# A depthwise convolution of 31 taps: VectorE's taps of the first and last channel group summed in SBUF, and the taps of a few groups shared out anew

## The reference

```
def _conv_module(h, w1, b1, wdw, bdw, lng, lnb, w2, b2):
    a, gt = jnp.split(h @ w1 + b1, 2, axis=-1)
    u = a * jax.nn.sigmoid(gt)
    u = lax.conv_general_dilated(
        u, wdw[:, None, :], window_strides=(1,),
        padding=[(CONV_WIDTH_2 // 2, CONV_WIDTH_2 // 2)],
        dimension_numbers=('NWC', 'WIO', 'NWC'),
        feature_group_count=u.shape[-1]) + bdw
    u = jax.nn.silu(_layernorm(u, lng, lnb))
    return u @ w2 + b2
```

## Time and profile before

| | us |
|---|---|
| median of 3 runs | 2614.68 (2612.6 to 2616.1) |
| the profiled execution's own time | 2617.16 |
| its span, first to last instruction | 2615.1 |
| TensorE busy | 2499.9 (96%) |
| VectorE busy | 1745.0 (67%) |
| ScalarE busy | 1092.4 (42%) |
| GpSimd busy | 366.2 (14%) |

### The profile page before, as it was taken

One profiled execution on the slowest core, in us unless ns is written; L12 is line 12 of the kernel. 1 busy time (PEld: TensorE's weight loads), 2 busy tenths in 40 slices (PEclk: granted clock), 3 DMA queues, 4 the chain that ended last, 5 costly groups with the idle time before them and its releaser, 6 DMA issues.

```text
span 2615.1 us, 35165 instructions
## 1 busy us (share of the span) xinstructions
PE 2499.9 (96%) x13498; PEld 2089.6 (80%) x13498; DVE 1745.0 (67%) x2562; ACT 1092.4 (42%) x1876; POOL 366.2 (14%) x414
## 2 busy tenths in 40 slices
PE   4999999999999999999989999999999999999998
PEld 3678987779979878877648887888888888777997
DVE  6967986858995776776865565675565665345454
ACT  3466544556554212236644322224322224334543
POOL 1101101001111100104831110100100100000101
PEclk9999999989999999999989999999999999999999
DMA  7645885536783554542102343453352443321462
GB/s 302 217 174 176 292 304 198 189 133 210 242 275 113 185 185 151 183 165 73 65 17 81 113 174 116 161 176 107 113 185 105 175 163 113 97 73 65 162 196 94
DMA packets 118293, 413.01 MB, mean 158 GB/s; under 512 B 13552, under 2 KB 17776, under 8 KB 118128
## 3 DMA queue, kind: packets, MB, share of 16 engines
q1 hardware_dynamic: 117568, 409.06, 44.9%
q10 hardware_dynamic: 560, 1.72, 0.2%
HBM read 409.68 MB, written 1.05 MB: 157 GB/s over the span
## 4 chain that ended last, share of the span: by engine, by line
PE 62%; DVE 4%; ACT 2%; issue 1%; POOL 1%; DVEq 0%; POOLq 0%; ACTq 0%
PE ps L1102 18%; PE ps L1104 18%; PE ps L1103 18%; PE ps L1318 2%; PE ps L1295 1%; PE ps L1255 1%; PE ps L1286 1%; DVE sl L1673 1%; DVE F L1790 1%; PE ps L1266 1%; DVE mjunk L1687 1%; POOL ap L2184 1%; ACT F L1440 1%; DVE ps L2027 0%; PE ps L1341 0%
## 5 line engine op out<-in xcount | busy, mean ns | idle before, releaser
L1102 PE MATMUL ps<-hH,sh 128*128 128x256 f32 (+1 forms) x2560 | 842.4, 329 | 6.9 <-DVE hL L1761 3.5
L1103 PE MATMUL ps<-hL,sh 128*128 128x256 f32 (+1 forms) x2560 | 835.7, 326 | 0.0
L1104 PE MATMUL ps<-hH,sl 128*128 128x256 f32 (+1 forms) x2560 | 835.6, 326 | 0.0
L1673 DVE TENSOR_TENSOR sl<-raw,sh 128x1024 fp32r<-128x1024 f32 x534 | 649.5, 1241 | 92.2 <-ACT sh L1381 91.6
L1381 ACT ACTIVATE sh<-raw 128x1024 fp32r<-128x1024 f32 x534 | 540.4, 1039 | 391.4 <-PE ps L1104 323.9
L1687 DVE CUSTOM_DVE_ANT_0 mjunk<-raw,cB,V 128x1024 bf16<-128x1024 f32 x384 | 539.1, 1404 | 29.9 <-DMA C<-in_cst 8.3
L1102 PEld LDWEIGHTS ps<-hH,sh 128*128 128x128 f32 x2560 | 482.3, 188 | 59.6 <-issue 8.5
L1104 PEld LDWEIGHTS ps<-hH,sl 128*128 128x128 f32 x2560 | 481.4, 188 | 48.2
L1103 PEld LDWEIGHTS ps<-hL,sh 128*128 128x128 f32 x2560 | 480.9, 188 | 48.7 <-issue 1.7
L2157 POOL TENSOR_TENSOR uLl<-F,uHh 128x256 fp32r<-128x256 f32 (+1 forms) x132 | 166.3, 1260 | 1203.0 <-ACT uHh L1562 1103.4
L1102 PE MATMUL ps<-sh,uHh 128*128 128x512 f32 x792 | 314.7, 397 | 10.5 <-DVE sl L1673 10.3
(11 more groups left out here) (168 smaller groups left out, 2250.5 us busy)
## 6 DMA issues: line engine op xcount, KB each, us to landing
raw<-in_w SPq DMA_DIRECT2D x756, 512.0 KB, 4.5
raw<-in_w SPq DMA_DIRECT2D x16, 256.0 KB, 3.8
cB<-in_rpb SPq DMA_DIRECT2D x64, 64.0 KB, 2.6
X<-in_x ACTq DMA_DIRECT2D x1, 1024.0 KB, 11.8
X<-in_ctx SPq DMA_DIRECT2D x1, 1024.0 KB, 7.4
out<-X SPq DMA_DIRECT2D x2, 512.0 KB, 2.7
raw<-in_w SPq DMA_DIRECT2D x2, 288.0 KB, 5.7
cB<-in_c ACTq DMA_DIRECT2D x1, 512.0 KB, 5.5
```

Source lines behind the costliest of these rows:

```text
L1102: self.e.matmul(out, lh, rh, start=start, stop=False)
L1103: self.e.matmul(out, lh, rl, start=False, stop=False)
L1104: return self.e.matmul(out, ll, rh, start=False, stop=stop)
L1673: self.e.tensor_tensor(lo[:, 0:w], raw[:, 0:w], hi[:, 0:w].bitcast(F32), ALU.subtract).then_inc(self.sems["w_lo"], 1)
```

## The change

For groups 0 and 7 (`APART`) VectorE no longer adds its taps onto TensorE's PSUM bank. The first tap is a multiplication of `UP` by the weight into `CB` (a `tensor_scalar`), the others add onto `CB`, with `UP` and `CB` both in SBUF. These taps wait for `UP` only, not for TensorE's taps. At the end there are two additions in place of one: `CB` + bank, then + `ap`.

Group 7's share goes from (13, 5) to (13, 8): ScalarE and GpSimd take three more taps, VectorE 9 in place of 12. `FIRST` (the number of ScalarE's rows that are issued in the group's own turn) goes from 7 to 4 for group 0, from 7 to 5 for group 1, and from 5 to 8 for group 7, whose rows are all issued there.

```
-SHARE = [(5, 11)] * 2 + [(6, 10)] * 4 + [(7, 9), (13, 5)]
+SHARE = [(5, 11)] * 2 + [(6, 10)] * 4 + [(7, 9), (13, 8)]
 HL_V = (0, 3, 5, 7)
-FIRST = [7] * 7 + [5]
+FIRST = [4, 5] + [7] * 5 + [8]
+APART = (0, 7)
...
     def tap_v(self, s):
 
         c, up, cid = s["c"], self.buf(s["up"]), s["cid"]
-        acc = cut(self.buf(s["b"])[:, 0:1], [[256, 2], [1, 256]])
-        self.wait_ge(self.got("full", s["b"]))
+        first = sum(SHARE[c]) + 1
+        if c in APART:
+            acc = self.m["CB"][:, c, :, :]
+            self.wait_ge(self.got("up", cid, c))
+        else:
+            acc = cut(self.buf(s["b"])[:, 0:1], [[256, 2], [1, 256]])
+            self.wait_ge(self.got("full", s["b"]))
         for k in s["ks"]:
-            if k > sum(SHARE[c]) + 1:
+            if k > first:
                 self.wait_ge(self.own("v_ps"))
+            if c in APART and k == first:
+                self.e.tensor_scalar(acc, up[:, :, k:k + 256], self.vec("conv_w_dw_2", (0, k), c), None,
+                                     ALU.mult).then_inc(self.sems["v_ps"], 1)
+                self.done("v_ps")
+                continue
...
         if s["ks"].stop < 31:
             return
         self.wait_ge(self.own("v_ps"))
+        if c in APART:
+            self.wait_ge(self.got("full", s["b"]))
+            self.e.tensor_tensor(self.flat(c), self.buf(s["b"])[:, :], self.flat(c), ALU.add).then_inc(
+                self.sems["v_ps"], 1)
+            self.done("v_ps", ("left", s["b"]))
+            self.wait_ge(self.own("v_ps"))
+            self.wait_ge(self.got("ap", cid, c))
+            self.e.tensor_tensor(self.flat(c), self.flat(c), self.buf(s["ap"])[:, :], ALU.add).then_inc(
+                self.sems["v_sb"], 1)
+            self.done("v_sb", ("left", s["ap"]), ("left", s["up"]), ("ct", cid, c))
+            return
```

## The result

The changed kernel takes 2619.72 us (median of 20 runs, 2613.7 to 2625.56) against 2614.57 before (20 runs, 2610.87 to 2617.25). The ratio is 1.0017 with a 95% interval of 1.0011 to 1.0023: slower by 4.4 us (2.9 to 6.0). That is clear of no change, and just inside the 0.2% that I had set as what can be told. The forecast was 2620.7.

A forecast was written before the change was run, and what follows sets the result against it. TensorE sets the pace, busy 96% of the span, so only its waits matter. 7.35 + 0.5 - 1.8 = +6.05 us on the profiled 2617.16 gives 2623.2, the median 2.5 below: 2620.7; range 2605 to 2626.

The forecast's parts named there:

- The likeliest case: Whole kernel: VectorE's two-SBUF-input taps and GpSimd's adds go by turns; +6.05 us, giving 2620.7; chance 0.60.
- L1674 ahead of group 2's `UP`: VectorE's instruction between group 1's taps and group 2's `UP`, expected to be blocked again and take 1.78 us.
- TensorE later at group 2's taps: Group 2: late `UP` makes TensorE start its taps 7.35 us later, after standing 11.4 us.
- The clock: Behind group 2's longer idle time: half clock for 5.8 to perhaps 9 us, costing 0 to 1.6; taken as 0.5.
- The price of a tap: Taps with `UP` and `CB` in SBUF beside adds: bounded by 0.79 and 1.76 us, taken at 1.76.
- The rival without blocking: Two-SBUF-input taps run at 0.79 beside adds; 0.4 won early, 5.7 and 2.7 late: -8.8 us, 2605.9; chance 0.17.
- VectorE first: VectorE's next tap passes GpSimd's waiting add: +3.8 front, -2.6 end, 0.4 clock, +1.6 us, 2616.3; chance 0.15.
- The front: Group 0 to group 2's `UP`: slowed taps make TensorE start group 2's taps 7.35 us later.
- Fewer early rows: Groups 0 and 1: ScalarE reaches group 2's sigmoid two adds sooner, worth nothing; without slowed taps up to 1.5 us.
- The end: Group 7: four taps by turns, four at 0.79, two additions; last mean matmul starts 1.8 us earlier.
- slower by over 0.2%: Outcome above 2619.9 us, beyond what a measurement can tell from no change; chance 0.49.
- no change that can be told: Outcome within 0.2%, from 2609.5 to 2619.9 us; chance 0.34.

The follow-up runs named there:

- e7: The changed kernel with `FIRST` 7 for groups 0 and 1, as before the change: 2620.81 us, ratio 1.0019 to the kernel before.
- e10: One run, for a trace, of the changed kernel with only group 0 summed in SBUF, group 7 as before the change: 2621.99 us, ratio 1.0026.
- e4: The changed kernel with the taps of groups 0 and 7 summed in a spare PSUM bank in place of `CB`: 2606.13 us, ratio 0.9970.
- e8: The changed kernel with a GpSimd memset of the row buffer in place of each add for groups 0 and 1: 2609.22 us, ratio 0.9974.
- e6: The kernel before with only group 7's share changed to (13, 8) and its `FIRST` to 8: 2614.56 us, ratio 0.9990.
- e3: The changed kernel with no sum in SBUF, groups 0 and 7 on TensorE's bank, shares and `FIRST` as changed: 2611.28 us, ratio 0.9983.
- e1: The changed kernel with group 0's taps back on TensorE's PSUM bank: 2612.44 us, ratio 0.9991.

## Why the prediction was right

The likeliest case came: VectorE and GpSimd by turns, a late `UP` of group 2, and a smaller gain at the end. The steps, in us behind t0 where they are times:

| step | predicted | measured |
|---|---|---|
| the multiplication into `CB` | 0.49 | 0.48 |
| a blocked tap and its add | 1.76 | 1.69 |
| `UP` of group 1, start | 10.8 | 10.34 |
| group 0's taps done | 26.6 | 25.64 |
| L1674 ahead of group 2's `UP` | 1.78 | 1.29 |
| `UP` of group 2, start | 36.2 | 34.48 |
| TensorE later at group 2's taps | +7.35 | +5.59 |
| the clock behind it | +0.5 | -1.4 (e7 -0.1, e10 -0.9) |
| the end | -1.8 | -2.13 |

- **The price of a tap** was bounded by 0.79 and 1.76 and taken at the upper bound, from the nearest row. It is 1.69. The blocked tap ends 0.55 after the add, not 0.61. e4 and e8 are the proof: take away the second SBUF input of VectorE, or the SBUF reading of GpSimd, and the same taps are at 0.79. The rival without blocking is out; so is "VectorE first", since the waiting add always went next.
- **The front** was sized 1.75 too high: 13 x 0.07 = 0.9 from the price, and 0.5 from L1674, which happened to meet the end of an add (1.29) where I had carried over a blocked one; the rest is spread over the rows between.
- **The clock** term had the wrong sign. I took the 5.8 us at half clock of the earlier trace rows as the least that could follow a longer idle time. In this execution it was 3.0, in e10, with 11.20 us of idle, 3.7 (the taps took 7.36), and in e7, with 11.03 us, 5.5 (the taps took 8.20). How long the clock had been down doesn't order them: by 1234.3 in the changed kernel, 7.3 us ahead of the taps, and by 1235.7 in e7, 8.0 us ahead of them, yet it stayed down longer in e7. It differs by execution, no fixed term describes it, and why is open.
- **Fewer early rows** I had costed at nothing because VectorE covers them, and so it is, nearly (34.48 against 34.75 in e7). Without the slowed taps I had allowed them up to 1.5; they bring 0.85 (e6 to e3).
- **The end** came as worked out, four taps blocked and four not. What I did not work out is what the shares alone would do: 2.38 (e3, 21.70 - 19.32). I credited the sum in SBUF with a gain that it doesn't make.

Summed up, the trace of the changed kernel has the last mean 2.0 us later behind t0 than before (139.60 against 137.58), and the terms with their measured values give 5.6 - 1.4 - 2.1 = +2.1, which says no more than that nothing else moved in between. At the end of the span 0.4 of it are left (2613.7 - 1206.29 = 1407.4 against 2615.1 - 1208.13 = 1407.0). The timed runs say +4.4 (2.9 to 6.0). The other clock outcome, as in e7, adds 1.4. The remainder is not settled: the profiled execution was a fast one of a kernel whose 20 runs spread over 12 us, against 6 for the 20 before, but beside e1 to e4 the kernel before spread over 13 as well (2609.86 to 2622.88), so a greater spread isn't shown. That the longer idle time gives the clock more room is a guess.

So the mechanism was right, and the closeness of the number (2620.7 against 2619.72) is in part luck: the terms as this trace has them, put on the same median of 2614.7, would have given 2616.8.

For the chances: 0.49 lay on slower by over 0.2% and 0.34 on no change that can be told. The ratio of 1.0017 lies inside the bound, so the outcome with the smaller of these two chances came; its whole interval is above 1, and its upper end of 1.0023 is beyond the bound.

## What to carry to other kernels

An accumulator in SBUF turns a VectorE multiply-add into one with two SBUF inputs; while GpSimd runs adds on SBUF, each then costs both engines a turn (1.69 us for a tap and an add here, against 0.79 from tap to tap). If the aim is only not to wait for TensorE's bank, take a spare PSUM bank: the same early start, at full speed. And before an overlap is credited with a gain, work out what the shares changed with it bring alone.

## What the runs showed of the hardware

- The blocking is for the reading only: 0.75 for a tap beside a memset of the same 128 x 512 buffer, 1.64 beside an add (e8). "SBUF — State Buffer" of the Trainium skill, section "Who interferes with whom", says just this, that such an instruction doesn't contend with one that only writes SBUF; the trace agrees.
- The single-input multiplication into `CB` took 0.48 from SBUF to SBUF (group 0), 0.60 where it began while GpSimd was ending an add (group 7), and 0.75 from SBUF into PSUM (e4).
- After an idle time of about 11 us the granted clock was 0.50 for the first 3.0, 3.7 and 5.5 us of work in three executions, and the first 12 matmul passes took 6.84, 7.36 and 8.20.
